# In the S5 stage, partition swap and Toeplitz table made by TensorE instead of copies and DMAs

## What is computed

```
bu_re = einsum('btgc,gpc->btgp', ug, bb_re)      # 32 groups g of 16 channels c, 64 modes p
bu_im = einsum('btgc,gpc->btgp', ug, bb_im)
h_t   = lambda * h_(t-1) + bu_t                  # complex, over time t (an associative scan)
y     = einsum(h_re, c_re) - einsum(h_im, c_im) + d * u
y     = gelu(y);  y = y * sigmoid(y @ w_glu)
```

## Time and profile before

| | |
|---|---|
| median of 3 runs | 2322.43 us (2315.08, 2322.43, 2325.42) |
| the profiled execution | 2315.08 us |
| its span in the profile | 2313.0 us, so 2.08 us lie outside it |
| PE busy in the span | 2215.1 us, 96% |
| DVE, ACT, POOL busy | 1168.0, 604.5, 279.6 us |
| S5 stage (PE) | from about 165 us to about 325 us |

### The profile page before, as it was taken

How to read it: one execution, slowest core, us unless ns; L and a number is a source line. 1 busy time by engine, 2 the same in 40 slices (tenths; PEclk the granted TensorE clock), 3 DMA queues, 4 the chain that set the end, 5 groups by cost and what they waited for, 6 DMA issues and landing times.

```text
span 2313.0 us, 34191 instructions
## 1 busy us (share of the span) xinstructions
PE 2215.1 (96%) x14592; PEld 2157.2 (93%) x14592; DVE 1168.0 (50%) x1283; ACT 604.5 (26%) x743; POOL 279.6 (12%) x432
## 2 busy tenths in 40 slices
PE   5799999999999999999999999999999999999995
PEld 5699999998999999999999988999999999999995
DVE  4717654444454354235643234446656665655665
ACT  4423233234212322233322034221111111111112
POOL 5989800000000000000000000000000000000000
PEclk9899999999999999999999999999999999999997
DMA  6311124123222222334322143111111111111111
GB/s 236 111 47 65 43 67 170 57 85 137 93 85 74 83 85 74 127 121 174 123 78 73 55 164 152 49 48 55 46 47 46 47 46 46 47 46 46 46 41 74
DMA packets 48004, 191.46 MB, mean 83 GB/s; under 512 B 5616, under 2 KB 7984, under 8 KB 44272
## 3 DMA queue, kind: packets, MB, share of 16 engines
q1 hardware_dynamic: 35216, 119.36, 15.3%
q0 software_dynamic: 10784, 53.29, 6.1%
q10 hardware_dynamic: 1872, 16.83, 1.9%
HBM read 152.53 MB, written 35.93 MB: 81 GB/s over the span
## 4 chain that ended last, share of the span: by engine, by line
PE 88%; DVE 4%; issue 3%; ACT 2%; POOL 1%; DMA 1%; DVEq 0%; ACTq 0%; POOLq 0%
PE ps L269 25%; PE ps L270 25%; PE ps L272 25%; PE ps L1773 1%; PE ps L2117 1%; PE ps L2093 1%; PE ps L2127 1%; DVE GT L424 1%; POOL W L685 1%; DVE WL L263 1%; ACT TMP L415 0%; DVE T L879 0%; PE ps L989 0%; ACT WH L258 0%; PE ps L990 0%
## 5 line engine op out<-in xcount | busy, mean ns | idle before, releaser
L269 PE MATMUL ps<-XH,WH 128*128 128x344 f32 x1704 | 549.3, 325 | 6.0 <-ACT STAGE L324 2.5
L270 PE MATMUL ps<-XL,WH 128*128 128x344 f32 x1512 | 480.6, 321 | 0.0
L269 PE MATMUL ps<-XN,WH 128*128 128x344 f32 x1248 | 399.0, 322 | 4.7 <-issue 4.2
L270 PE MATMUL ps<-XN,WH 128*128 128x344 f32 x1248 | 396.9, 321 | 0.0
L263 DVE TENSOR_TENSOR WL<-WRAW,WH 128x1024 fp32r<-128x1024 f32 x177 | 222.7, 1258 | 298.7 <-ACT WH L258 297.9
L272 PE MATMUL ps<-XH,WL 128*128 128x344 f32 x1704 | 362.0, 321 | 0.0
L269 PEld LDWEIGHTS ps<-XH,WH 128*128 128x128 f32 x1704 | 322.0, 189 | 16.6 <-issue 11.1
L258 ACT ACTIVATE WH<-WRAW 128x1024 fp32r<-128x1024 f32 x177 | 186.4, 1054 | 531.2 <-PE ps L272 517.3
L270 PEld LDWEIGHTS ps<-XL,WH 128*128 128x128 f32 x1512 | 286.2, 189 | 0.1
L272 PEld LDWEIGHTS ps<-XH,WL 128*128 128x128 f32 x1704 | 286.0, 189 | 0.0
L272 PE MATMUL ps<-XN,WL 128*128 128x344 f32 x1248 | 264.0, 319 | 1.7 <-issue 1.6
(11 more groups left out here) (516 smaller groups left out, 3089.5 us busy)
## 6 DMA issues: line engine op xcount, KB each, us to landing
WRAW<-in_wslabs SPq DMA_DIRECT2D x177, 512.0 KB, 3.5
scratch_spill<-STAGE SPq DMA_DIRECT2D x40, 516.0 KB, 2.7
ZS<-scratch_spill POOLq DMA_DIRECT2D x24, 516.0 KB, 5.3
XIN<-in_xT POOLq DMA_DIRECT2D x1, 4128.0 KB, 18.2
XR<-in_xT ACTq DMA_DIRECT2D x2, 2064.0 KB, 9.1
out_y<-XR SPq DMA_DIRECT2D x8, 516.0 KB, 3.0
CACHES<-in_ck ACTq DMA_DIRECT2D x4, 1024.0 KB, 14.2
CACHES<-in_cv ACTq DMA_DIRECT2D x4, 1024.0 KB, 15.6
```

The source lines that it names most:

```text
L269: pe.matmul(out[t], WH[:, slot, w, :], xh(k, t), start=(k == 0), stop=False)
L270: pe.matmul(out[t], WH[:, slot, w, :], xl(k, t), start=False, stop=False)
```

## The change

Three things are changed in each quarter, and the fill steps are distributed anew.

- A second weight matrix BT2 (the halves of BT1 exchanged, one negated) is made by two ACT copies; PE multiplies U by it too, so the exchanged input stands in PSUM banks 5 and 6. DVE's turn before the scan becomes two products and a subtraction, all of 128 partitions.
- After the scan PE multiplies EP by a constant matrix PSW that exchanges the halves with the sign, two matmuls of 512 columns. ACT's two copies (859) go. DVE's product EP times RC comes ahead of the fill's WL.
- PE makes the Toeplitz blocks, eight matmuls with shifted pieces of an identity (SHIFT) as weights and GK moving, and one ACT copy brings them to TT. SP's DMAs, their semaphore and the MEMSET go.
- The constants CF grow from four 128x128 blocks to five.
- A quarter had 1, 2, 5, 5, 2, 1 fill steps at points a, b, c, d, f, g. It now has 3, 2, 3, 2, 2, 2, 2 at a, b, c, d, e, f, g, where e is new and lies between the Toeplitz matmuls and the sample product. Both add up to 16, and slabs are still completed at c and g.
- The semaphore for one GpSimd result is a new one (s5_den) instead of the second count of s5_red.

```
-        (("a", 1), ("b", 2), ("c", 5), ("d", 5), ("f", 2), ("g", 1))]
+        (("a", 3), ("b", 2), ("c", 3), ("d", 2), ("e", 2), ("f", 2), ("g", 2))]
...
-        CF = cst("CF", [128, 4, 128])
+        CF = cst("CF", [128, 5, 128])
+        SHIFT = CF[:, 0:2, :].rearrange("p a i -> p (a i)")
...  sp_weights
-            def toeplitz(q):
-                sp.wait_ge(s5_zero, 1)
-                sp.wait_ge(s5_act, s5_out("gk", q + 1))
-                for t in range(8):
-                    o_ = 16 * (7 - t)
-                    sp.dma_start(TT[0:128 - o_, t, :], GK[o_:128, :]).then_inc(tt_in, 16)
...  act_s5
+                nc.scalar.activation(BT2[:, :, 0:64], two(5)[:, :, 64:128], ACT.Copy, scale=-1.0).then_inc(s5_act, 1)
+                nc.scalar.activation(BT2[:, :, 64:128], two(5)[:, :, 0:64], ACT.Copy).then_inc(s5_act, 1)
...
-                act.wait_ge(s5_scan, q + 1)
-                for h in range(2):
-                    nc.scalar.activation(ps[64 * h:64 * h + 64, 5:7, :],
-                                         EP[64 - 64 * h:128 - 64 * h, :, :].rearrange("p (a g) n -> p a (g n)", a=2),
-                                         ACT.Copy, scale=2.0 * h - 1.0).then_inc(s5_act, 1)
...
+                act.wait_ge(s5_pe, s5_at("tt", q + 1))
+                nc.scalar.activation(TT[:, :, :].rearrange("p g (t c) -> p t g c", c=16),
+                                     two(3).rearrange("p t (g c) -> p t g c", c=16), ACT.Copy).then_inc(s5_act, 1)
+                act_fill(act, f"s{q}e")
...  dve_s5
-            nc.vector.memset(TT[:, :, :], 0.0).then_inc(s5_zero, 1)
...
-                tt(r4(T4[:, 0]), bu, r4(rc[:, :, :]), M)
-                for h in range(2):
-                    tt(part(r4(T4[:, 1]), h), part(bu, 1 - h), part(r4(rs[:, :, :]), 1 - h), M)
-                L(nc.vector.scalar_tensor_tensor(out=T4[:, 0], in0=T4[:, 1], scalar=SGN, in1=T4[:, 0], op0=M, op1=AD))
+                tt(r4(T4[:, 0]), b2(3), r4(rc[:, :, :]), M)
+                tt(r4(T4[:, 1]), b2(5), r4(rs[:, :, :]), M)
+                tt(T4[:, 0], T4[:, 0], T4[:, 1], SU_)
...  (the scan)
+                tt(T4[:, 0], EP[:, :, :], rc[:, :, :], M)
                 dve_fill(dve, f"s{q}c")
-                tt(T4[:, 0], EP[:, :, :], rc[:, :, :], M)
-                dve.wait_ge(s5_act, s5_out("swap", q + 1))
+                dve_fill(dve, f"s{q}d")
+                dve.wait_ge(s5_pe, s5_at("swap", q + 1))
...  pe_s5
-                    last = pe.matmul(ps[:, 3 + g // 4, c], BT1[:, g, :], U[:, g, :], start=True, stop=True)
+                    pe.matmul(ps[:, 3 + g // 4, c], BT1[:, g, :], U[:, g, :], start=True, stop=True)
+                    last = pe.matmul(ps[:, 5 + g // 4, c], BT2[:, g, :], U[:, g, :], start=True, stop=True)
...  (after point d)
+                pe.wait_ge(s5_scan, q + 1)
+                for k in range(2):
+                    last = pe.matmul(ps[:, 5 + k, :], PSW, EP[:, 4 * k:4 * k + 4, :].rearrange("p g n -> p (g n)"),
+                                     start=True, stop=True)
+                last.then_inc(s5_pe, 1)
+                pe.wait_ge(s5_act, s5_out("gk", q + 1))
+                for t in range(8):
+                    last = pe.matmul(two(3)[:, t, :], SHIFT[:, 16 * (7 - t):16 * (7 - t) + 128], GK[:, :],
+                                     start=True, stop=True)
+                last.then_inc(s5_pe, 1)
+                pe_fill(pe, f"s{q}e")
...
-                pe.wait_ge(tt_in, 128 * (q + 1))
+                pe.wait_ge(s5_act, s5_out("tt", q + 1))
```

More of the change, by code:

```diff
@@ L165, in cst @@
             return t
-        CF = cst("CF", [128, 4, 128])
-        IDENT, MASKNEG, ONES = (CF[:, k, :] for k in (0, 2, 3))
+        CF = cst("CF", [128, 5, 128])
+        IDENT, MASKNEG, ONES, PSW = (CF[:, k, :] for k in (0, 2, 3, 4))
+        SHIFT = CF[:, 0:2, :].rearrange("p a i -> p (a i)")
         LVL = cst("LVL", [128, LEVELS, 128], U8, 1)
@@ L239, in sp_weights @@
                 slab(j)
[L240 to L245, removed]
             assert (N_SLABS - first) % 2 == 0 and first % 2 == 1
@@ L562, in dve_mem @@
             dve_project(dve, SL_CK, 8)
-            dve.wait_ge(s5_red, 2)
+            dve.wait_ge(s5_den, 1)
             nc.vector.reciprocal(W(14), W(11)).then_inc(s5_rec, 1)
@@ L656, in program @@
         EP = USU
-        BT1 = nxt("BT1", [128, 8, 128])
+        BT1, BT2 = nxt("BT1", [128, 8, 128]), nxt("BT2", [128, 8, 128])
         TT, HST = nxt("TT", [128, 8, 128]), nxt("HST", [128, 8, 128])
@@ L665, in program @@
         T4 = at("T4", [128, 2, 8, 128], O_TMP)
-        s5_rec, pool_step = sem("s5_rec"), sem("pool_step")
+        s5_den, s5_rec, pool_step = sem("s5_den"), sem("s5_rec"), sem("pool_step")
         s5_in, s5_exp, s5_red, s5_sin = sem("s5_in"), sem("s5_exp"), sem("s5_red"), sem("s5_sin")
@@ L669, in program @@
         s5_act = sem("s5_act")
-        s5_out = counts("tok0", "tok", "decay", "gk", "u", "bt", "st", "su", "swap0", "swap", "y0", "y", "ys")
+        s5_out = counts("tok0", "tok", "decay", "gk", "u", "bt1", "bt2", "bt", "st", "su", "tt", "y0", "y", "ys")
         s5_zero = sem("s5_zero")
@@ L677, in program @@
         s5_pe = sem("s5_pe")
-        s5_at = counts("tok", "bt", "gk", "u", "s", "st", "su", "ss", "y", "yt", "ys", "yst")
-        s5_stored, tt_in = sem("s5_stored"), sem("tt_in")
+        s5_at = counts("tok", "bt", "gk", "u", "s", "st", "su", "swap", "tt", "ss", "y", "yt", "ys", "yst")
+        s5_stored = sem("s5_stored")
         W = lambda k: W32[:, k, :] if k < 17 else WP[:, k - 17, :]
@@ L725, in pool_s5_prepare @@
             tt(W(12), li, li, M)
-            nc.gpsimd.tensor_tensor(W(11), W(11), W(12), AD).then_inc(s5_red, 1)
+            nc.gpsimd.tensor_tensor(W(11), W(11), W(12), AD).then_inc(s5_den, 1)
             pool.wait_ge(s5_rec, 1)
@@ L830, in act_s5 @@
                 else:
-                    act.wait_ge(s5_zero, 2)
+                    act.wait_ge(s5_zero, 1)
                     act.wait_ge(s5_tables, 1)
@@ L880, in dve_s5 @@
             M, AD, SU_ = ALU.mult, ALU.add, ALU.subtract
-            nc.vector.memset(TT[:, :, :], 0.0).then_inc(s5_zero, 1)
             nc.vector.memset(HST[:, :, 0:1], 0.0).then_inc(s5_zero, 1)
-            dve.wait_ge(s5_zero, 2)
+            dve.wait_ge(s5_zero, 1)
             for q in range(4):
@@ L891, in dve_s5 @@
                 dve.wait_ge(s5_pe, s5_at("s", q + 1))
+                b2 = lambda k: ps[:, k:k + 2, :].rearrange("p a (g n) -> p a g n", n=128)
                 r4 = lambda x: x.rearrange("p (a g) n -> p a g n", a=2)
-                part = lambda x, h: x[64 * h:64 * h + 64]
-                bu = ps[:, 3:5, :].rearrange("p a (g n) -> p a g n", n=128)
-                tt(r4(T4[:, 0]), bu, r4(rc[:, :, :]), M)
-                for h in range(2):
-                    tt(part(r4(T4[:, 1]), h), part(bu, 1 - h), part(r4(rs[:, :, :]), 1 - h), M)
-                L(nc.vector.scalar_tensor_tensor(out=T4[:, 0], in0=T4[:, 1], scalar=SGN, in1=T4[:, 0], op0=M, op1=AD))
+                tt(r4(T4[:, 0]), b2(3), r4(rc[:, :, :]), M)
+                tt(r4(T4[:, 1]), b2(5), r4(rs[:, :, :]), M)
+                tt(T4[:, 0], T4[:, 0], T4[:, 1], SU_)
                 dve.wait_ge(s5_act, s5_out("decay", q + 1))
@@ L903, in dve_s5 @@
                 dve.wait_ge(s5_scan, q + 1)
+                tt(T4[:, 0], EP[:, :, :], rc[:, :, :], M)
                 dve_fill(dve, f"s{q}c")
-                tt(T4[:, 0], EP[:, :, :], rc[:, :, :], M)
-                dve.wait_ge(s5_act, s5_out("swap", q + 1))
-                tt(r4(T4[:, 1]), ps[:, 5:7, :].rearrange("p a (g n) -> p a g n", n=128), r4(rs[:, :, :]), M)
+                dve_fill(dve, f"s{q}d")
+                dve.wait_ge(s5_pe, s5_at("swap", q + 1))
+                tt(r4(T4[:, 1]), b2(5), r4(rs[:, :, :]), M)
                 if q:
@@ L912, in dve_s5 @@
                 tt(SOUT[:, gs, 0], T4[:, 0, :, 127], T4[:, 1, :, 127], AD)
-                dve_fill(dve, f"s{q}d")
+                dve_fill(dve, f"s{q}e")
                 dve.wait_ge(s5_pe, s5_at("ss", q + 1))
@@ L985, in pe_s5 @@
                 last.then_inc(s5_pe, 1)
-                pe.wait_ge(tt_in, 128 * (q + 1))
+                pe.wait_ge(s5_act, s5_out("tt", q + 1))
                 for g in range(8):
                     c = slice((g % 4) * 128, (g % 4) * 128 + 128)
-                    pe.matmul(ps[:, 3 + g // 4, c], U[:, g, :], TT[:, :, 16 * g:16 * g + 16], start=True, stop=False)
+                    pe.matmul(ps[:, 3 + g // 4, c], U[:, g, :], TT[:, g, :], start=True, stop=False)
                     last = pe.matmul(ps[:, 3 + g // 4, c], HST[:, g, 0:128],
@@ L2620, in lay_out @@
                                   gate, slabs(f["w_out"][0]), slabs(f["w_cq"][0]), slabs(f["w_co"][0])] + ffn, 0)
-    cf = z((128, 4, 128), np.float32)
+    cf = z((128, 5, 128), np.float32)
     r = np.arange(128)
@@ L2626, in lay_out @@
     cf[:, 3] = 1
+    cf[64 + np.arange(64), 4, np.arange(64)] = -1
```

(1 more changed line is left out.)

## The result

| | before | after |
|---|---|---|
| median | 2322.51 us (2315.08 to 2325.42) | 2352.96 us (2348.65 to 2354.97, 4 runs) |
| ratio to before, 95% interval | | 1.0136 [1.0111, 1.0160] |
| profiled execution | 2315.08 us | 2361.72 us |
| S5 stage, first transposes to GLU | 328.24 - 165.37 = 162.9 us | 347.92 - 167.55 = 180.4 us |
| GLU to FFN | 1284.4 us | 1294.1 us |

The forecast was 2338 us, +15.5, in a range up to 2347. Measured is +30.5, outside the range. The direction was right, and so was the sum for the S5 stage. What it lacks lies 1.3 ms later, in a loop whose source text the change does not touch.

The account below looks back on a forecast made before the run. PE, busy 96% of the span, was taken to bound the kernel. 21.1 + 1.2 - 1.35 - 4.9 - 0.6 = +15.5 us on the median 2322.43 gave 2338 us, 0.67% slower, range 2328 to 2347.

Parts of the forecast that it names:

- Work of PE: S5 stage, four quarters: added float32 matmuls (BT2 7.1 us, Toeplitz 7.1, exchange 6.8) cost 21.1 us that nothing hides.
- one-pass rival: New S5 matmuls go as one record instead of two, 8.9 us in all; total +3.3, 2325.7 us; chance 0.04.
- Wait for BT2: PE waits before the mode inputs for ACT's two new copies: 0.3 us a quarter, 1.2 in all.
- no half clock behind it: Rival denied: BT2 wait brings its own half clock ahead of the mode inputs; +22 to +27 us, chance 0.11.
- No wait for the scan or TT: PE reaches the exchange 0.9 us after the scan; ACT's TT copy (1.0 us) lies beside point e; no wait.
- STAGE: PE's waits after point c for ACT to copy a finished slab stay at 2.5 us.
- End: PE's 3.1 us wait for the GLU input shrinks by 0.5 to 0.6 through a second fill step at g.
- HST and clock: Wait before the sample product falls from 2.7 to 1.35 us; half clock in quarters 0 to 2 goes, -4.9.
- The term of 4.9 us: Half clock at the output product, 1.63 us a quarter in quarters 0 to 2, disappears; called the least certain term.
- The sum of the stage: S5 stage: added work and waits less the savings make +15.5 us.
- that is 2330.5: Whole program: the +15.5 us put on the profiled execution of 2315.08 us.

Follow-up runs that it names:

- run 2: The changed kernel, measured once more with nothing changed: 2354.40 us, ratio 1.0148 to the kernel before.
- run 1: The kernel before, measured once more with nothing changed: 2320.83 us, ratio 0.9995.
- run 8: The kernel before with one line moved, DVE's product of EP with RC ahead of the fill's WL: 2317.74 us, ratio 0.9996.
- run 9: The changed kernel with PE's FFN loop written out, so without branches back: 2326.59 us, ratio 1.0035 to the kernel before.
- run 10: The kernel before with PE's FFN loop written out, so without branches back: 2312.93 us, ratio 0.9974.
- run 3: The kernel before with 32 semaphore increments that nobody waits for ahead of PE's program: 2341.95 us, ratio 1.0093.
- run 12: The kernel before with 64 semaphore increments that nobody waits for ahead of PE's program: 2315.14 us, ratio 0.9978.

## Why the prediction was wrong

Step by step, against the timelines after. PE, quarter 0:

```profile
179.54 0.46 PE L960 MATMUL ps<-U,BT 128*128 128x128 f32 x2 [0.27 <-ACT BT L836]
...
183.18 0.27 PE L963 MATMUL ps<-CF,SU 128*8 128x128 f32 x1
...
191.84 1.88 PE L972 MATMUL ps<-USU,CF 128*128 128x512 f32 x4
193.55 1.95 PE L977 MATMUL ps<-GK,CF 128*128 128x128 f32 x16
195.26 0.40 PE L256 MATMUL ps<-XH,WH 128*128 128x344 f32 x1
...
199.87 0.47 PE L990 MATMUL ps<-TT,U 128*128 128x128 f32 x2
...
203.44 0.40 PE L256 MATMUL ps<-XH,WH 128*128 128x344 f32 x1
```

DVE and then ACT, quarter 0:

```profile
186.00 1.22 DVE L869 TENSOR_TENSOR T<-T 128x1024 f32<-128x1024 f32 x1
187.26 3.14 DVE L888 TENSOR_TENSOR_SCAN USU<-HST,T 128x1024 f32<-128x1024 f32 x1
...
195.95 1.70 DVE L898 TENSOR_TENSOR HST<-T 128x1016 f32<-128x1016 f32 x1
```

```profile
178.77 0.62 ACT L836 ACTIVATE BT<-ps 128x512 f32<-128x512 f32 x1
...
195.54 1.03 ACT L852 ACTIVATE TT<-ps 128x1024 f32<-128x1024 f32 x1 [5.70 <-PE ps L977]
```

- *Work of PE: right.* Exchange 193.55 - 191.84 = 1.71 us, shifts 195.26 - 193.55 = 1.71, mode inputs 183.18 - 179.54 = 3.64 where they were 1.78. In a quarter 5.28, in all 21.1, as forecast. The one-pass rival is out: two products of 512 columns took 1.71 us. By the rule of the Trainium skill (TensorE: Matmul & The Clock Gate, section Back-to-back issue gap) they would take 0.43, an estimate; the trace has its pace for this kernel's float32r products (0.23 us each), not for its float32 ones.
- *Wait for BT2: right*, 1.0 us for 1.2, and no half clock behind it (mode inputs at 0.23 a matmul).
- *No wait for the scan or TT: right.* In quarter 0 the scan ends at 190.40, 1.4 us ahead of PE, where 0.9 was forecast. The subtraction, taken as 2.0 us, was 1.22 us in quarters 0, 1 and 3 and 2.24 in quarter 2, where the scan is only 0.5 us ahead. TT is there 3.3 us early.
- *STAGE: right*, 2.5 us. *End: half right*, 3.1 became 2.8, not 2.5.
- *HST and clock: right in kind, too certain in size.* One wait of 1.1 us is left, in quarter 2, behind the slow subtraction (none at all in run 2), and only there is the output product at part half clock, 5.2 us; in quarter 0 it takes 203.44 - 199.87 = 3.57, as the earlier trace rows have it without a wait. The term of 4.9 us was read from one execution, and the wait for POOL that takes its place when HST's is short (runs 1 and 8) was in no rival. It decides little here: the half clock that before loses to either wait is 5 to 7 us.
- *The sum of the stage: right*, within what profiles differ by. 21.1 + 1.0 - 1.6 (HST) - 3.3 (two half clock stretches fewer) - 0.3 = +16.9 by these rows; 17.5 between the two profiled executions, 13.5 between the means of five and four profiles, 13.7 between the medians of runs 9 and 10, and 15.5 was forecast.
- *What failed* is the step that had no line of its own: "that is 2330.5", where the stage's sum was put on the whole program as if all other code stayed as it was. What the new instructions do to the loop behind them was put at nothing, without a line. The 144 new matmul and 144 weight load records stand ahead of PE's loop; they move it by 32 within a block, and each of its four branches back then costs (15.7 - 5.8) / 4 = 2.5 us more in wait and, by the 17.5 us of the FFN, some 1.9 us in half clock behind it. Run 3 gives this term alone, 20.8 us (18 of them in the FFN); 15.5 + 20.8 = 36, and 13.7 + 19.2 (FFN: 686.1 and 688.5 against 668.6 and 667.6) = 33, against the 30.5 measured and 33.2 of run 2 (2354.40 - 2321.18).

The waits for issue were in the trace of before, 4.2 us at four heads of one loop and 1.6 us behind them, small enough to pass over. They were the sign that PE's instructions can cost time beside their execution, and the change adds 288 of them ahead of that loop.

Left open: why 32 is a bad place and 0, 64, 160 and 256 are good ones; that PE waits for code there is the likeliest reading, but no view names it. Only the place was varied, not the length of the loop. PE's other loops (lines 341, 584 and 1839 of the kernel before) have no wait for issue in any profile, which is not explained either.

## What to carry to other kernels

Where an engine that bounds has a loop, look for its waits for issue at the loop's head and count by how many instructions an edit ahead of it moves the loop: here 32 cost 0.9%, and with the loop written out those waits were gone and the kernel before won 0.26%. Time an edit with the loop written out, or with a pad that keeps its place, or its cost is mixed with that of the place. Check that the pad fits into a time in which the engine idles: 224 increments did not. And work on the bounding engine that stands where it would wait costs less than its time: here taking one piece of about 7 us back did not shorten the stage in any of three trials, and lengthened it in two.

## What the runs showed of the hardware

- In this loop a branch back of PE came with a wait of 0.7 to 1.7 us in the good places (one in run 12 with none in the view) and of 3.7 to 4.6 us in the bad one, the same code else. Behind each of the twelve long waits (after, runs 2 and 3) the granted clock fell to 0.50, which is 1.2 GHz, for 3 to 6 us; behind none of the short ones did it fall.
- PE takes at most 0.16 us for an increment of a semaphore: 224 of them end at 35.4 us.
- Half clock came behind waits for HST of 0.74, 0.94 and 0.99 us (before), 1.13 us (after), 1.15 us (run 12) and 1.15 and 1.23 us (run 10), each with the sample product of 8 columns behind it, and not behind the same wait of 0.20 and 0.61 us (run 1) or 0.39 us (run 9). In run 3 it came behind one of 0.56 us and not behind one of 0.59, so the length of the wait does not decide alone. Behind waits for issue of up to 1.68 us, with fill matmuls of 344 columns after them, the clock stayed full.
- A DVE subtraction of two SBUF tiles of 1024 elements took 1.22 us in three quarters and 2.24 in the fourth (after), and 1.23 to 2.12 in run 2, mostly under the nearest rows, 1.87 and 2.33. The HST sum took 1.70 us in quarters 0 to 2 of after and 1.22 in run 2, where it was 2.06 to 2.33 before.
